# Two-layer decoder step on one core: x loaded in fourths, an early root table, a later turn of sample weights, and one more place for layer two's experts

## The reference

```python
h = x
for i in range(2):
    h = h + mixer_i(rmsnorm(h, norm_mix[i]))      # 0: convolution, 1: latent attention
    h = h + hier_moe(rmsnorm(h, norm_ffn[i]), ...)
    h = h + (p[i] @ ple_w_in[i]) * sigmoid(rmsnorm(h, ple_g[i]) @ ple_w_gate[i])
y = rmsnorm(h, norm_final)
# hier_moe: sum over a token's two experts of gate * (silu(h @ w_gate) * (h @ w_up)) @ w_down
```

## Time and profile before

| | us |
|---|---|
| median of 3 runs | 812.29 (810.41 to 816.27) |
| the profiled execution | 812.26 |
| its span, first to last instruction | 810.2 |
| PE busy in it | 737.2 (91%) |
| DVE, ACT, POOL busy | 343.1, 208.5, 55.3 |
| moved by DMA | 270.64 MB, mean 334 GB/s |

### The profile page before, as it was taken

How to read it: one execution, slowest core, us unless ns; L and a number is a source line. 1 busy time by engine, 2 the same in 40 slices (tenths; PEclk the granted TensorE clock), 3 DMA queues, 4 the chain that set the end, 5 groups by cost and what they waited for, 6 DMA issues and landing times.

```text
span 810.2 us, 16399 instructions
## 1 busy us (share of the span) xinstructions
PE 737.2 (91%) x6292; PEld 525.6 (65%) x6292; DVE 343.1 (42%) x1012; ACT 208.5 (26%) x498; POOL 55.3 (7%) x99
## 2 busy tenths in 40 slices
PE   7999999999899769899999889989999798688894
PEld 5886677766566436658875556768666465466483
DVE  3578624433333213236466564252333132313345
ACT  2100324421111111133236462154211121111232
POOL 1501000000000000000071800000000000000000
PEclk9999999999999989999999999999999899989998
DMA  9873895999999999999188656994999999999901
GB/s 358 350 226 79 294 423 205 336 421 423 417 420 423 419 421 420 414 422 406 70 281 306 206 161 261 421 407 168 422 420 419 419 421 420 420 419 417 370 1 53
DMA packets 64064, 270.64 MB, mean 334 GB/s; under 512 B 7776, under 2 KB 18224, under 8 KB 44016
## 3 DMA queue, kind: packets, MB, share of 16 engines
q1 hardware_dynamic: 57680, 259.72, 80.1%
q10 hardware_dynamic: 3408, 5.25, 2.0%
q0 software_dynamic: 2896, 4.58, 1.9%
HBM read 262.44 MB, written 3.61 MB: 328 GB/s over the span
## 4 chain that ended last, share of the span: by engine, by line
PE 49%; DMA 20%; DVE 5%; SPq 5%; ACT 2%; issue 2%; ACTq 0%; DVEq 0%
PE bank L634 14%; PE bank L774 11%; DMA ring<-in_moe_w_up 11%; PE bank L748 7%; DMA arena<-in_moe_w_up 6%; PE bank L803 4%; SPq L2250 3%; PE bank L817 3%; DMA ring<-in_moe_w_down 2%; DMA arena<-in_moe_w_down 2%; PE bank L1107 1%; PE bank L942 1%; SPq L2240 1%; PE bank L1132 1%; PE bank L1063 1%
## 5 line engine op out<-in xcount | busy, mean ns | idle before, releaser
L774 PE MATMUL bank<-ring,arena 128*32 128x256 f32 x1344 | 114.3, 408 | 14.9 <-DMA ring<-in_moe_w_up 10.7
L634 PE MATMUL bank<-xn_sq,ring 128*128 128x264 f32 x480 | 108.3, 387 | 2.4 <-issue 1.4
L748 PEld LDWEIGHTS bank<-arena 128*128 128x128 f32 x864 | 99.0, 192 | 9.2 <-issue 9.1
L634 PEld LDWEIGHTS bank<-xn_sq,ring 128*128 128x128 f32 x480 | 90.9, 190 | 19.4 <-issue 2.7
L634 PE MATMUL bank<-arena,ring 128*128 128x264 f32 (+1 forms) x440 | 103.0, 389 | 0.2
L748 PE MATMUL bank<-arena 128*128 128x128 f32 (+1 forms) x864 | 102.6, 277 | 0.5 <-DVE arena L1440 0.5
L1472 DVE TENSOR_TENSOR arena<-arena,bank 128x128 f32<-128x128 f32 x34 | 9.8, 288 | 218.2 <-ACT arena L1921 218.2
L774 PEld LDWEIGHTS bank<-ring,arena 128*32 128x32 f32 x1344 | 61.4, 117 | 53.1 <-issue 30.2
L634 PEld LDWEIGHTS bank<-arena,ring 128*128 128x128 f32 x440 | 81.9, 190 | 18.5 <-issue 3.8
L774 PE MATMUL bank<-xn_sq,arena 128*32 128x256 f32 x384 | 52.5, 435 | 19.7 <-DMA ring<-in_moe_w_up 19.7
L1490 DVE TENSOR_TENSOR hT<-hT,bank 128x264 f32<-128x264 f32 x144 | 61.6, 429 | 18.8 <-PE bank L828 10.1
(11 more groups left out here) (280 smaller groups left out, 870.2 us busy)
## 6 DMA issues: line engine op xcount, KB each, us to landing
ring<-in_stream SPq DMA_DIRECT2D x34, 1024.0 KB, 14.4
ring<-in_moe_w_gate SPq DMA_DIRECT2D x34, 1024.0 KB, 18.4
ring<-in_moe_w_up SPq DMA_DIRECT2D x34, 1024.0 KB, 20.8
ring<-in_moe_w_down SPq DMA_DIRECT2D x28, 1024.0 KB, 21.9
arena<-in_moe_w_down SPq DMA_DIRECT2D x24, 1024.0 KB, 22.3
arena<-in_moe_w_gate SPq DMA_DIRECT2D x14, 1024.0 KB, 20.1
arena<-in_moe_w_up SPq DMA_DIRECT2D x14, 1024.0 KB, 21.1
xn_sq<-in_moe_w_gate SPq DMA_DIRECT2D x12, 1024.0 KB, 20.2
```

The source lines that it names most:

```text
L634: t = mm(ps[:, 0:cols], lhs(k), rhs(k), start=(k == 0), stop=(k == n - 1))
L748: t = mm(bank[k // 4][:, (k % 4) * n:(k % 4 + 1) * n], XR[:, i, k * P:(k + 1) * P], S[:, j % 2, i, 0:n], start=(i == 0), stop=(i == 2))
L774: t = mm(bank[2 + r][p0:p0 + U, 0:F].rearrange("p (c f) -> p c f", c=2), x, w[i][:, :, k * F + c * P:k * F + (c + 1) * P], start=(k == 0), ...
```

## The change

- **Start.** ACT's queue loads x in four parts ahead of the constants; SP loads the first piece in four parts. PE runs six matmuls on the constant, then first_pair: kind 0 of chunks 0 and 1 together, k by k, with one more such matmul ahead of k = 2, 4, 6. added_squares comes after kind 1 of chunk 0. Vector taps count on s_dve instead of a semaphore of their own, and s_p, s_wr and s_back share others.
- **Attention.** The turn of the new tokens' weights and its copy move from sample_weights and sample_turned to sample_values and sample_rows.
- **Layer two's pins.** PIN_LAST has three instead of five, PIN_INSIDE five instead of three, and these come after down(0) instead of before it. Chunks 0 to 2 go to late_pins and are stored by SP ahead of its wait for s_perm; window_in(0) of layer two waits for that store; SP reads them back into pin0 after the first piece of the last gate's weights. Chunks 3 to 7 go to pin0.
- **Places.** Layer two has the park among its down places and the late order of layer one, in which (7, 2) comes second; RING_LAST stands before (9, 2) instead of (8, 2).
- **End.** embed(1) makes ACT take a root of one element ahead of the last square.

```diff
-    _dn = (SHELF, *((PARK,) if _l == 0 else ()), *(x[2] for x in _gu))
+    _dn = (SHELF, PARK, *(x[2] for x in _gu))
...
-            [(6, 2), (6, 0), (6, 1), (7, 0), (7, 1), (8, 0), (8, 1), (7, 2), (8, 2), (9, 2), (9, 0), (9, 1)]]
+            [(6, 2), (7, 2), (6, 0), (6, 1), (7, 0), (7, 1), (8, 0), (8, 1), (8, 2), (9, 2), (10, 2), (9, 0), (9, 1)]]
...
-PIN_LAST = [(7,), (0, 1, 2, 3, 4)]
-PIN_INSIDE = [(), (5, 6, 7)]
+PIN_LAST = [(7,), (0, 1, 2)]
+PIN_INSIDE = [(), (3, 4, 5, 6, 7)]
...
+            def first_pair():
+
+                ps = [open_bank(pe, ("pw1", 0, c)) for c in range(2)]
+                w = slot(G_PW1).rearrange("p (k f) -> p k f", k=KD)
+                for k in range(KD):
+                    if k in (2, 4, 6):
+                        mm(bank[7][:, 0:T], rstd[:, 0:P], rstd[:], start=True, stop=True)
+                    if k % 2 == 0 and k < 6:
+                        pe.wait_ge(s_w0[k // 2], 16)
+                    if k == 6:
+                        landed(pe, G_PW1)
+                    pe.wait_ge(s_xn, k + 1)
+                    for c in range(2):
+                        t = mm(ps[c][:, 0:T], w[:, k, c * P:(c + 1) * P], xnT[:, k, :], start=(k == 0),
+                               stop=(k == KD - 1))
+                        if k == KD - 1:
+                            t.then_inc(is_full(("pw1", 0, c)), 1)
+                expand(0, (1,))
+                added_squares("n0")
+                expand(1, (1,))
...
-                        pin_inside()
-                    down(a)
+                    down(a)
+                    if j == 0:
+                        pin_inside()
...
+            def sample_values(B):
                 ps = open_bank(pe, ("sn", B))
                 pe.wait_ge(t_pn, B + 1)
                 tr(ps[0:TS, 0:P], pnew, ident).then_inc(is_full(("sn", B)), 1)
-            def sample_values(B):
...
+                freed(pe, ("sn", B))
                 mm(ps[:, 0:KL], PTn, ckR[0:TS, :], start=False, stop=True).then_inc(is_full(("sv", B)), 1)
...
-                    if j == 0 and l == 0:
-                        dve.wait_ge(s_spill[1], 16)
+                    if j == 0:
+                        dve.wait_ge(s_spill[1], 16 * (l + 1))
...
+            for i in range(4):
+                act.dma_start(hT[:, 2 * i:2 * i + 2, :], a["xT"][:, 2 * i:2 * i + 2, :]).then_inc(s_x[i], X_IN)
             act.dma_start(cst[:, 0:C_IOTA], a["constants"][:, 0:C_IOTA]).then_inc(s_cst, 16)
...
-                for m in PIN_INSIDE[l]:
-                    pin_in(l, m)
...
                     pair_out(a)
+                    if j == 0:
+                        for m in PIN_INSIDE[l]:
+                            pin_in(l, m)
...
+                    if l and m == KD:
+                        s.activation(early_root[:], ones[0:1, 0:1], ACT.Sqrt)
                     if m:
                         act.wait_ge(s_ple, KD * l + m)
...
+                else:
+                    freed(sp, ("pin", 1, KD - PIN_EARLY - 1))
+                    sp.dma_start(spill[:, 0:KD - PIN_EARLY], late_pins).then_inc(s_spill[1], 16)
                 sp.wait_ge(s_perm, l + 1)
...
-            for g in range(G_PG1, NPIECE):
+            fill(G_PG1)
+            sp.wait_ge(s_spill[1], 32)
+            sp.dma_start(pin0[:, 0:KD - PIN_EARLY], spill[:, 0:KD - PIN_EARLY]).then_inc(s_back, 16)
+            for g in range(G_PG1 + 1, NPIECE):
                 fill(g)
```

More of the change, by code:

```diff
@@ L401, in build @@
             w_in[i] = w_in[j]
[L402 to L405, removed]
+        s_x = [sem("in_" + n) for n in ("x0_then_p", "x1_then_router", "x2", "x3")]
+        s_p, s_wr = s_x[0:2]
+        X_IN = 16
+        s_w0 = [sem(f"in_first_piece{i}") for i in range(3)]
+        s_cst, s_vec, s_dw, s_pg = (sem("in_" + n) for n in ("cst", "vec_then_pins_back", "taps_and_state", "pages"))
         s_tab = sem("in_tables_and_taps_by_block")
@@ L570, in _ @@
             pe.wait_ge(s_dve, 1)
-            for _ in range(7):
+            for _ in range(6):
                 mm(bank[7][:, 0:T], rstd[:, 0:P], rstd[:], start=True, stop=True)
-            pe.wait_ge(s_cst, 16)
             def sum_squares(key, src, n, base):
@@ L585, in added_squares @@
                 ps = open_bank(pe, key)
+                pe.wait_ge(s_cst, 16)
                 pe.wait_ge(s_acc, sum(ADDED[key]))
@@ L635, in chunk, with expand @@
                 t.then_inc(is_full(key), 1)
-            def expand(c):
-                for kind in range(2):
+            def expand(c, kinds=(0, 1)):
+                for kind in kinds:
                     g = G_PW1 + 2 * (c // 2) + kind
                     w = slot(g).rearrange("p (k f) -> p k f", k=KD)
[L641 to L650, removed]
-                    chunk(("pw1", kind, c), KD, lambda k: w[:, k, (c % 2) * P:(c % 2 + 1) * P],
-                          lambda k: xnT[:, k, :], wait=wait)
-                    if c == 0 and kind == 0:
-                        added_squares("n0")
+                    landed(pe, g)
+                    chunk(("pw1", kind, c), KD, lambda k: w[:, k, (c % 2) * P:(c % 2 + 1) * P],
+                          lambda k: xnT[:, k, :])
+            def first_pair():
[17 more added lines that the diff above has]
+                expand(1, (1,))
             def taps(p, cs=(0, 1)):
@@ L683, in means @@
                 mm(ps[:, 0:T], ones, zT[:, KD - 1, :], start=False, stop=True).then_inc(is_full("lnm"), 1)
-            for c in range(KD):
+            first_pair()
+            for c in range(2, KD):
                 expand(c)
@@ L1838, in h_ready @@
                 return lambda k: freed(act, key + (k,))
-            squares("n0", hT, 4, lambda k: act.wait_ge(s_x[0], 16))
-            act.wait_ge(s_x[1], 16)
+            squares("n0", hT, 4, lambda k: act.wait_ge(s_x[k // 2], X_IN))
             act.dma_start(wq, a["tapsQ"]).then_inc(s_tab, 16)
@@ L1845, in _ @@
             act.dma_start(stT, a["stateT"]).then_inc(s_dw, 16)
-            squares("n0", hT[:, 4:KD], 4, lambda k: act.wait_ge(s_x[1], 16), at=4)
+            squares("n0", hT[:, 4:KD], 4, lambda k: act.wait_ge(s_x[2 + k // 2], X_IN), at=4)
+            act.wait_ge(s_cst, 16)
             root("n0")
@@ L2278, in expert_stream @@
                         number[e] = sp.value_load(permI[0:1, e:e + 1], min_val=0, max_val=E - 1)
-                    if l == 1 and (e, c) == (8, 2):
+                    if l == 1 and (e, c) == (9, 2):
                         load_expert(l, *RING_LAST, RING_LAST[0])
@@ L2289, in _ @@
             sp.dma_start(vt[:], a["vectors"]).then_inc(s_vec, 16)
-            for hf in range(2):
-                ks, fs = slice(4 * hf, 4 * hf + 4), slice(SLOT // 2 * hf, SLOT // 2 * (hf + 1))
-                sp.dma_start(hT[:, ks, :], a["xT"][:, ks, :]).then_inc(s_x[hf], 16)
+            for i in range(4):
+                fs = slice(SLOT // 4 * i, SLOT // 4 * (i + 1))
                 sp.dma_start(slot(G_PW1)[:, fs], a["stream"][G_PW1][:, fs])\
-                    .then_inc(w_in[PLACE[G_PW1]] if hf else s_w0, 16)
+                    .then_inc(s_w0[i] if i < 3 else w_in[PLACE[G_PW1]], 16)
             for g in range(1, NSLOT):
```

39 lines of the change are left out of this document (21 added, 18 removed).

## The result

Predicted 804.0 us (801.5 to 808.8), measured 809.25 us (median of 13 runs, 803.55 to 815.13) against 813.85 for the kernel before in the same comparison: ratio 0.9933, 95% interval 0.9905 to 0.9961. By the ratio that is 5.4 us less, by the two medians 4.6, where 8.25 were forecast. On the base that the forecast worked from it makes 812.26 x 0.9933 = 806.8 us, inside the range; the median itself lies 0.45 us above it. The changed kernel was measured a second time among the experiments: 806.66 us (6 runs, 803.35 to 808.47) against 815.23, ratio 0.9893 (0.9858 to 0.9927), 8.7 us less.

The account below looks back on a forecast made before the run. Expert layers were taken as bound by the DMA stream of 1 MB pieces, elsewhere PE and short waits. Start 2.85, attention 2.3, layer two 2.7 and end 0.4 sum to 8.25; 812.26 less that gives 804.0 us (801.5 to 808.8).

Parts of the forecast that it names:

- The start: PE's expansion at the kernel's start: its last matmul ends at 65.0 instead of 67.85, 2.85 us sooner.
- six constants end at 5.82: PE's start: six matmuls on the constant end at about 5.82 us, and the real ones follow without pause.
- Rival 3: At the start, fourths come no earlier than halves, so the start gives only 1.0: 805.9 us; chance 0.14.
- Attention: PE's waits of 1.42 and 1.56 us for the new tokens' weights go; 1.3 and 1.0 kept, together 2.3 us.
- one short wait: Sign in attention: both waits for the new tokens' weights gone, one short PE wait at the second block's end.
- Layer two: Layer two's pins and places: 1.78 from an earlier gather(0), 2.51 from a parked piece, less 1.55 standing dry: 2.7 us.
- the dry gap: Layer two's weight stream: DMA stands dry once for 1.55 us, 20 us after the restart, awaiting down(1).
- the supply: Layer two: eight pieces issuable before SP stands at (9, 2) flow until 579.45, while down(1) ends at 580.0.
- Rival 1: Layer two: supply holds, pairs 0 and 1 done by 578, DMA never dry: 802.5 us; chance 0.13.
- rival 2: Layer two gives nothing, through an equally long dry gap or a late store: 806.7 or 808.0 us; chance 0.17.
- Rival 4: Layer two: PE's clock might stay at 1.2 GHz through fillers, gather(0) and pair 0, 10.6 us more: 814.6; chance 0.06.
- The end: Last root in embed(1): its table load moves into ACT's idle time ahead of the last square, 0.4 us sooner.

Follow-up runs that it names:

- three constants: The changed kernel with three constant matmuls instead of six ahead of the first real ones at the start: ratio 0.9943, 808.91 us.
- the first with attention's fillers: The changed kernel with three constant matmuls in PE's 1.50 us pause ahead of head 14's weights, first of two measurements: ratio 0.9858, 803.92 us.
- The parts alone: The start, the late turn of the new tokens' weights, and layer two's pins, places and order, each alone on the kernel before: 0.9949, 0.9971, 0.9957.

## Why the prediction was right, and where not

**The base.** I worked from the profiled 812.26 and called it the median. Over the comparisons the kernel before had medians of 813.85, 814.45, 815.14, 814.24 and 815.23: the profiled execution lay some 2 us under its own median. Its rows fit that: the clock fell neither at layer one's routing nor in its embed stage, where it did in others. This is 1.6 of the 5.2 us between 804.0 and the first measured median, and 3.0, more than the whole of 2.7, at the second.

**The start, forecast 2.85.** One pair of profiles misleads here: by the first, 1.0 us was left, by the second 3.2. Over the ten profiles with this start and six constants the expansion ends at 65.40 on the mean (64.69 to 66.01), over the three without it at 67.97; the last pair's taps start at 80.46 and 83.11. So 2.6 us, and the copies take nothing back: PE's wait for them is 0.59 to 1.69 with the edit and 0.79 to 1.39 without. My step "six constants end at 5.82" failed: the first real matmul, which follows them at once, began between 5.75 and 6.83, at 6.47 on the mean, because the slow passes ended anywhere from 4.6 to 7.3. Rival 3 fell: x's first fourth was used by DVE at 3.99 (3.93 to 4.26 over the profiles), where half of x came at 5.42.

**Attention, forecast 2.3.** Measured with this part alone: 1.47 in the stretch with the first block's wait, 1.20 in the one with the second's, 2.67. The 1.20 stands in every profile (12.71 or 12.72 us in eleven with the turn, 13.92 in three without); the first stretch takes 121.2 to 121.4 in nine of the eleven, 122.8 to 122.9 in the three. Both terms were too small: in the first block the whole wait goes, not 1.3 of it, and in the second 1.20 go, not 1.0. The 0.28 us wait at the end of the second block is the "one short wait" of the prediction.

**Layer two, forecast 2.7.** The earlier gather came as worked out: from gather(0) to the first down product 16.2 us against my 16.26. The piece in the park gave its 2.5, the dry gap took 1.9 instead of 1.55 and came once, 22 us after the restart. From the counts to the stream's end the six profiles with these places have 216.5 to 219.2, on the mean 217.4, against 219.2 three times without them: 1.8. Four of the six have 216.8, which is 2.4 less, and that is 1.8 + 2.5 - 1.9. So one step that failed is the supply, whose gap was 0.35 longer than worked out, and the other is the clock, which I put into a rival and at nothing in the sum. Rival 1 fell, rival 2 too. Rival 4's place was right and its size wrong: in two of these six (three constants; the first with attention's fillers) the half clock went on through the pins, and gather(0) came 10.2 us after the counts instead of 8.67, 1.5 us lost and not 10.6. Windows of the run with attention's fillers, where 0.50 holds from 540 to 546 (in the first profile of the changed kernel it reads 0.50 from 550 to 552 and 0.66 from 552 to 554):

```profile
544.00:546.00 2.00, 2.00 (x6) 1.49 (x6) 1.83 (x11) 0.38 (x1) 0.00 (x0) 0.50 0.10 41
```

**The end, forecast 0.4.** Up to the reciprocal 0.4 came, 4.87 to 4.45. Up to the last instruction 0.24 were lost, 12.39 to 12.63 us from PE's last product: my sum stopped at the root and put what stands behind it, the stores of y, at no change without a reason, and the last of them lands 0.66 later. The Trainium skill's drain of 1.38 us per table load ("ScalarE: Activation LUTs", What ACT_TABLE_LOAD costs) is again not in the rows: the small root starts 0.02 us after its load has ended. What the Trainium skill says of queues ("Trainium Kernel Development and Optimization", Key Constraints) no run here tells apart, since x's move to ScalarE's queue was not tried without the fourths.

**The sum.** 2.6 + 2.67 + 1.8 + 0.4 - 0.66 = 6.8, against 8.25 forecast and 5.4 and 8.7 measured. That it lies within 1.5 of the forecast is in part luck: attention's term was 0.4 too small, and the start's, layer two's and the end's were 0.25, 0.9 and 0.65 too large. The parts alone gave 0.9949, 0.9971 and 0.9957, which multiply to 0.988, 10 us; their intervals are too wide to say that the parts hinder each other, and apart from the last store no stage shows it. What stays open is whether the changed kernel falls to half clock more often than the one before. Ten of fourteen profiles have a stretch between layer one's transposes and its gather (1.0 to 1.5 us), among them two of the four whose start is the old one or whose only edit is the start. PE's pause for "issue" in layer one (1.2 to 1.5 us, last section) stands in seven of the ten with the whole change and in one of the other four. These counts are too small to decide it.

## What to carry over

Read a stage's worth from several executions, by the distance between two points on one engine inside the stage; against a spread of 10 us between executions, two whole spans say little, while most of these distances repeated to 0.2 us or better where the clock had not fallen. And follow a gain to the last instruction: the 0.4 us won at the last root were lost again at the last store. Before work is moved behind the point where a queue's next issue waits, look for a pause ahead of it: two of the three pins that stood before gather(0) fitted into a 1.76 us wait and cost nothing there, unless the clock had fallen ahead of it (1.5 us in one execution).

## What was not expected of the hardware

- Two executions of one program differ by 8.8 us, and the traces put it down to places: a fall of the granted clock behind one 1.50 us pause of PE (12.1 instead of 8.9 us from the sample products to wo), another in the embed stage, slower first matmuls (0.9 us later), longer copies (1.1).
- At the start the passes take 0.44 us each at first and 0.22 later. The windows show a granted clock of 1.00 there, but the profile's record of the clock only begins at 7.24 us in the first profile of the changed kernel, at 5.04 in the second and at 9.08 with three constants, in all fourteen profiles within 0.4 us of the last slow pass, and a stretch ahead of the record is shown as 1.00. Where 0.50 is recorded, a pass of the same 264 columns takes 0.44 us too (542 to 546 in the run with attention's fillers). So the slow passes have the length of the lower level, 1.2 GHz; the record itself does not say which level held there. With a 1.33 us pause of PE in between they went on to 9.0 us; in the thirteen others they ended between 4.2 and 7.3.
- Behind an expert layer's branch PE stood 1.2 to 1.5 us for "issue" in some executions and not in others, at the same instruction:

```profile
349.70 1.60 PE L567 MATMUL bank<-cst 128*128 128x264 f32 x6
352.83 3.46 PE L838 MATMUL bank<-arena 64*128 64x264 f32 x16 [1.53 <-issue]
```

This is the second profile of the changed kernel in layer one; the kernel before has such a pause in layer two (1.21) and none here.
